# A two-block transformer kernel on one core: weights rounded in two halves of 1024 columns instead of one piece of 2048

## The reference, cut to what matters

```
def conv_ffn(h, w_up, conv_w, conv_b, w_down):
    u = h @ w_up
    ...
    return (jax.nn.silu(gate) * val) @ w_down

def swiglu(h, w13, w2):
    a, b = jnp.split(h @ w13, 2, axis=-1)
    return (jax.nn.silu(a) * b) @ w2
```

## Time and profile before

| | |
|---|---|
| median of 3 runs | 3355.73 us (3351.95 to 3360.63) |
| the profiled execution | 3357.11 us, of which its span (first to last instruction) is 3355.3 us |
| granted PE clock, mean | 0.995 of full |
| busy, share of the span | PE 98%, DVE 54%, ACT 37%, POOL 30% |
| weight loads | 298 of 1024 KB, median 4.8 us from issue to landing |

### The profile page before, as it was taken

How to read it: one execution, slowest core, us unless ns; L and a number is a source line. 1 busy time by engine, 2 the same in 40 slices (tenths; PEclk the granted TensorE clock), 3 DMA queues, 4 the chain that set the end, 5 groups by cost and what they waited for, 6 DMA issues and landing times.

```text
span 3355.3 us, 48284 instructions
## 1 busy us (share of the span) xinstructions
PE 3278.1 (98%) x17840; PEld 2804.2 (84%) x17840; DVE 1809.4 (54%) x2219; ACT 1247.2 (37%) x1627; POOL 1020.4 (30%) x505
## 2 busy tenths in 40 slices
PE   7989999999999999999999999999999999999999
PEld 6768888888888888998888877988888888998887
DVE  5467876553478766457645665664552255262222
ACT  4464333354444334443322445322242223442221
POOL 2112222221112222544434241343423332223332
PEclk9999999999999999999999999999999999999999
DMA  4202333321224333445544310454422243222222
GB/s 143 73 37 101 144 138 125 113 102 51 88 84 156 136 133 109 174 174 185 186 155 175 120 67 14 156 189 150 169 101 100 93 164 113 95 82 100 100 89 100
DMA packets 69901, 401.69 MB, mean 120 GB/s; under 512 B 7520, under 2 KB 10224, under 8 KB 31216
## 3 DMA queue, kind: packets, MB, share of 16 engines
q1 hardware_dynamic: 46400, 317.80, 26.2%
q10 hardware_dynamic: 23344, 81.73, 6.9%
HBM read 397.41 MB, written 2.10 MB: 119 GB/s over the span
## 4 chain that ended last, share of the span: by engine, by line
PE 90%; DVE 3%; ACT 3%; issue 2%; POOL 1%; DMA 1%; SPq 0%; DVEq 0%; ACTq 0%; POOLq 0%
PE banks L535 24%; PE banks L537 23%; PE banks L536 23%; PE banks L441 3%; PE banks L442 3%; PE banks L443 3%; PE banks L552 2%; PE banks L554 2%; PE banks L553 2%; ACT whi L970 1%; POOL wlo L2262 1%; PE banks L651 1%; DMA raw<-stream 1%; PE banks L886 1%; PE banks L873 1%
## 5 line engine op out<-in xcount | busy, mean ns | idle before, releaser
L2262 POOL TENSOR_TENSOR wlo<-raw,whi 128x512 fp32r<-128x512 f32 (+1 forms) x282 | 707.7, 2510 | 2025.7 <-ACT whi L970 2023.7
L535 PE MATMUL banks<-h_hi,whi 128*128 128x512 f32 (+1 forms) x2752 | 1040.2, 378 | 11.5 <-POOL wlo L2262 5.4
L536 PE MATMUL banks<-h_lo,whi 128*128 128x512 f32 (+1 forms) x2752 | 1034.2, 376 | 0.0
L537 PE MATMUL banks<-h_hi,wlo 128*128 128x512 f32 (+1 forms) x2752 | 1034.2, 376 | 0.0
L970 ACT ACTIVATE whi<-raw 128x2048 fp32r<-128x2048 f32 x281 | 536.9, 1911 | 527.8 <-PE banks L537 523.1
L1524 DVE TENSOR_TENSOR wlo<-raw,whi 128x1536 fp32r<-128x1536 f32 (+1 forms) x281 | 530.6, 1888 | 296.2 <-ACT whi L970 296.0
L535 PEld LDWEIGHTS banks<-h_hi,whi 128*128 128x128 f32 x2752 | 518.3, 188 | 112.2 <-issue 16.3
L536 PEld LDWEIGHTS banks<-h_lo,whi 128*128 128x128 f32 x2752 | 518.5, 188 | 94.3 <-issue 1.7
L537 PEld LDWEIGHTS banks<-h_hi,wlo 128*128 128x128 f32 x2752 | 518.5, 188 | 94.0
L535 PE MATMUL banks<-mid_hi,whi 128*128 128x512 f32 (+1 forms) x1136 | 424.6, 374 | 4.0 <-POOL wlo L2262 3.1
L536 PE MATMUL banks<-mid_lo,whi 128*128 128x512 f32 (+1 forms) x1136 | 424.0, 373 | 0.0
(11 more groups left out here) (287 smaller groups left out, 4029.6 us busy)
## 6 DMA issues: line engine op xcount, KB each, us to landing
raw<-stream SPq DMA_DIRECT2D x298, 1024.0 KB, 4.8
mraw<-mod_stream ACTq DMA_DIRECT2D x144, 512.0 KB, 3.4
x<-xT SPq DMA_DIRECT2D x8, 256.0 KB, 6.1
out<-x SPq DMA_DIRECT2D x8, 256.0 KB, 2.2
ka<-k_a ACTq DMA_DIRECT2D x1, 1600.0 KB, 8.6
ko<-k_odd ACTq DMA_DIRECT2D x1, 1152.0 KB, 5.3
crow<-c_rows ACTq DMA_DIRECT2D x1, 1024.0 KB, 7.1
cx<-ctxT SPq DMA_DIRECT2D x1, 1024.0 KB, 7.5
```

Source lines behind the costliest of these rows:

```text
L535: mm(o, hi, a_hi[:, kc, 0:T], start=(kc == 0), stop=False)
L536: mm(o, hi, a_lo[:, kc, 0:T], start=False, stop=False)
L537: last = mm(o, lo, a_hi[:, kc, 0:T], start=False, stop=(kc == K - 1))
L2262: G.tensor_tensor(wlo[:, slot, wd:], raw[:, slot, wd:], whi[:, slot, wd:].bitcast(F32), ALU.subtract)\
```

## The change

ACT rounds a slab in two instructions of 1024 columns each. The first raises a new semaphore `whi_half`, the second raises `whi_done`. POOL's part of `wlo` moves from the last columns to the first ones (0 to 511, in `ctx_ffn` 0 to 255) and waits for `whi_half` alone. DVE's part becomes two instructions: the rest of the first half (512 columns, in `ctx_ffn` 768) after `whi_half`, and the whole second half (1024 columns) after `whi_done`; `wlo_done` comes with the second. The same is done in `split_extra`. PE and SP wait for what they waited for before. The first two slabs of the program are rounded as before, only their columns are shared out anew. A DVE wait that was there twice goes.

```diff
+HW = SLAB // 2
...
-def dve_part(s):
+def pool_part(s):
     first, count = PLAN["ctx_ffn"]
-    return SLAB - (WPOOL // 2 if first <= s < first + count else WPOOL)
+    return WPOOL // 2 if first <= s < first + count else WPOOL
...
+        whi_half = sem("whi_half")
...
-                    A(whi[:, s % 2, :], raw[:, s % 2, :], ACT.Copy).then_inc(whi_done, 1)
+                    A(whi[:, s % 2, 0:HW], raw[:, s % 2, 0:HW], ACT.Copy).then_inc(whi_half, 1)
+                    A(whi[:, s % 2, HW:], raw[:, s % 2, HW:], ACT.Copy).then_inc(whi_done, 1)
...
                 if s + 2 < NSLAB:
+                    dve.wait_ge(whi_half, s + 1 + i2)
+                    dve.wait_ge(slab_done, s + 1 + i2)
+                    w = slice(pool_part(s), HW)
+                    V.tensor_tensor(wlo[:, s % 2, w], raw[:, s % 2, w], whi[:, s % 2, w].bitcast(F32), ALU.subtract)
                     dve.wait_ge(whi_done, s + 3 + i2)
-                    dve.wait_ge(slab_done, s + 1 + i2)
-                    w = slice(0, dve_part(s))
-                    V.tensor_tensor(wlo[:, s % 2, w], raw[:, s % 2, w], whi[:, s % 2, w].bitcast(F32),
+                    V.tensor_tensor(wlo[:, s % 2, HW:], raw[:, s % 2, HW:], whi[:, s % 2, HW:].bitcast(F32),
                                     ALU.subtract).then_inc(wlo_done, 1)
...
-            def split_w(slot, whi_at, done_at, wd=WD):
-                pool.wait_ge(whi_done, whi_at)
-                if done_at is not None:
-                    pool.wait_ge(slab_done, done_at)
-                G.tensor_tensor(wlo[:, slot, wd:], raw[:, slot, wd:], whi[:, slot, wd:].bitcast(F32), ALU.subtract)\
+            def split_w(slot, half_at, done_at, wd):
+                pool.wait_ge(whi_half, half_at)
+                pool.wait_ge(slab_done, done_at)
+                G.tensor_tensor(wlo[:, slot, 0:wd], raw[:, slot, 0:wd], whi[:, slot, 0:wd].bitcast(F32), ALU.subtract)\
                     .then_inc(wlo_pool_done, 1)
```

More of the change, by code:

```diff
@@ L988, in split_extra @@
                 act.wait_ge(raw_loaded[s % 2], 16 * (s // 2 + 1))
-                A(w_hi(s), raw[:, s % 2, :], ACT.Copy).then_inc(whi_done, 1)
+                A(w_hi(s)[:, 0:HW], raw[:, s % 2, 0:HW], ACT.Copy).then_inc(whi_half, 1)
+                A(w_hi(s)[:, HW:], raw[:, s % 2, HW:], ACT.Copy).then_inc(whi_done, 1)
             def load_ln_exp():
@@ L1533, in split_extra @@
             def split_extra(s):
+                dve.wait_ge(whi_half, s - 1)
+                V.tensor_tensor(w_lo(s)[:, WPOOL:HW], raw[:, s % 2, WPOOL:HW], w_hi(s)[:, WPOOL:HW].bitcast(F32),
+                                ALU.subtract)
                 dve.wait_ge(whi_done, s + 1)
-                V.tensor_tensor(w_lo(s)[:, 0:WD], raw[:, s % 2, 0:WD], w_hi(s)[:, 0:WD].bitcast(F32),
+                V.tensor_tensor(w_lo(s)[:, HW:], raw[:, s % 2, HW:], w_hi(s)[:, HW:].bitcast(F32),
                                 ALU.subtract).then_inc(wlo_done, 1)
@@ L1862, in _ @@
             dve.wait_ge(whi_done, 2)
-            V.tensor_tensor(wlo[:, 1, 0:WD], raw[:, 1, 0:WD], whi[:, 1, 0:WD].bitcast(F32), ALU.subtract)\
+            V.tensor_tensor(wlo[:, 1, WPOOL:], raw[:, 1, WPOOL:], whi[:, 1, WPOOL:].bitcast(F32), ALU.subtract)\
                 .then_inc(wlo_done, 1)
@@ L2249, in _ @@
             G = nc.gpsimd
-            WD = SLAB - WPOOL
             step = [0]
@@ L2320, in _ @@
                 .then_inc(wlo_pool_done, 1)
-            split_w(1, 2, None)
+            pool.wait_ge(whi_done, 2)
+            G.tensor_tensor(wlo[:, 1, 0:WPOOL], raw[:, 1, 0:WPOOL], whi[:, 1, 0:WPOOL].bitcast(F32), ALU.subtract)\
+                .then_inc(wlo_pool_done, 1)
             splits(slab_of("even_in"), 13)
```

14 lines of the change are left out of this document (6 added, 8 removed).

## The result

| | before | after |
|---|---|---|
| median | 3355.47 us (3351.95 to 3360.63, 4 runs) | 3333.9 us (3331.68 to 3336.98, 4 runs) |
| profiled execution | 3357.11 us | 3331.68 us |
| its span | 3355.3 us | 3329.9 us |
| granted PE clock, mean | 0.995 | 0.996 |

The ratio of the times is 0.9936, with a 95% interval of 0.9924 to 0.9949. The direction, the mechanism and most places were forecast; the size was not. The gain of 21.5 us is a third larger than the sum of 16.3 us, and 3333.9 lies 0.1 us under the low end of the range, 3334.0.

A forecast was written before the change was run, and what follows sets the result against it. PE, busy 3278.1 of 3355.3 us, was taken as the bound, so only its waits could be won. Terms summed to 16.3 us, giving 3340.8 from 3357.11; the forecast was 3340.5, range 3334 to 3350.

The forecast's parts named there:

- the down rounds of `ctx_ffn`: Rounds paced by a loop through three engines; each turn 0.5 us shorter, gaining 2.6 (first) and 3.2 (second and third).
- costs that did not come: Starts of attention stages, where PE waits with a rounding or split ahead: 0.1 to 0.3 us each, -0.8 in all.
- the up slabs: Up slabs of `ctx_ffn`: four PE waits, 3.0 us in all, nearly vanish as the chain shortens by 0.9; gain 2.9.
- the `halved` waits: Four PE waits of 0.8 us in `halved` stretches, 3.8 in all: gain 0.9 each, 3.6 us.
- The forecast chain of 3.7 in `ctx_ffn`: From ACT's start to the end of `wlo`: 3.7 us instead of 4.63; 0.9 us taken off each chain.
- 954 and 964: PE's wait of 2.2 us and the 4.1 us behind it, for `ss`: gain 1.5 us in all.
- the waits for `ss`: Four other PE waits for DVE's `ss`: POOL's blocking goes; gain 2.3 us, within bounds 0 and 3.6.
- The clock as a rival: Half-clock stretch near 963 and dip near 1523 go, winning 3 to 4 us more: 3337; chance 0.10.
- The rule on the lockout: Trainium skill: two-input DVE and POOL instructions exclude each other entirely; gain about 0.75 us a chain, time 3343.6.
- GpSimd comes last again: In the split chain, POOL gets the port only after DVE's second instruction; about 3348 us; chance 0.18.
- It gains nothing: PE's waits put down to POOL could be for something else landing at the same time: 3356 us; chance 0.05.
- VectorE's queue becomes the bound: Modulated conv layers: DVE's added waiting exceeds its 1.35 us idle a slab; 3361, up to 3370; chance 0.05.

The follow-up runs named there:

- e5: Kernel before, with ACT rounding in two halves but DVE (one instruction) and POOL (first columns) both waiting for the second: 3357.65 us, ratio 1.0010.
- e1: Kernel after, but DVE waits for the whole rounding and does its part in one instruction: 3331.55 us, ratio 0.9941.
- e4: Kernel after measured and profiled once more, without an edit: 3333.5 us, ratio 0.9942.
- e2: Kernel after, but DVE takes the whole first half and POOL the last columns, waiting for `whi_done`: 3340.23 us, ratio 0.9960.
- e3: Kernel after, but ACT rounds 512 then 1536 columns; POOL takes the first piece, DVE the second in one instruction: 3329.51 us, ratio 0.9933.
- e9: Kernel after with POOL's part cut from 512 columns to 64 (32 in `ctx_ffn`): 3330.61 us, ratio 0.9924.

## Why the prediction was right, and where it was not

**In sum.** Direction and mechanism were right, and three terms of the sum were mis-sized. Of the 9.1 us by which the steps exceed the sum (25.4 less 16.3) 3.1 are the clock's and 0.9 the first load's, which the medians don't show in full. The rest is in the down rounds of `ctx_ffn` (1.9), in two waits put at nothing (1.5) and in costs that did not come (1.2); what is left nearly cancels (0.4 and 0.4 too little for the up slabs and `ss`, 0.5 too much for the `halved` waits). These three make 4.6 of the 5.2 us by which the medians' gain of 21.5 exceeds 16.3.

**Right: what bounds the kernel, and the chain.** PE does not wait in the 512-token feed-forward layers, before or after the earlier trace rows; most of the 25.4 us lies at the places of rows 2 and at their like. The forecast chain of 3.7 in `ctx_ffn` is 3.72, that of 4.0 with 512 columns is 4.01 in `ffn00`; in the conv layers it is 4.52, and no wait shows it. The order of the turns (DVE, POOL, DVE) holds, and e5 and e1 show that POOL's turn inside the rounding brings the gain by itself. The waits before lines 535 and 441, forecast at 3 and 1.5 us, are 2.3 and 1.4.

**Right: four waits of `halved` stretches, 954 and 964, the waits for `ss`.** 3.6, 1.5 and 2.3 us were forecast, and the steps are 3.1, 1.6 and 2.7. The steps for `ss` also settle the choice within 0 and 3.6: near the upper bound, where it was taken, and that choice had little behind it.

**Failed step: the down rounds of `ctx_ffn`.** 2.6 and 3.2 were forecast, 3.4 and 4.2 came. The prediction made the loop 0.5 us shorter, to 6.2 a turn (one slab), and took it for the bound in every slab. In the timeline of the first round after (the rows of rows 6):

```profile
1439.10 0.87 DVE L1659 SCALAR_TENSOR_TENSOR cx<-banks,gates,cx 128x256 f32<-128x256 f32 x2
...
1444.69 1.05 ACT L972 ACTIVATE whi<-raw 128x1024 fp32r<-128x1024 f32 x1
...
1445.22 0.87 DVE L1659 SCALAR_TENSOR_TENSOR cx<-banks,gates,cx 128x256 f32<-128x256 f32 x2
1446.00 1.37 DVE L1526 TENSOR_TENSOR wlo<-raw,whi 128x768 fp32r<-128x768 f32 x1
1447.29 1.21 DVE L1528 TENSOR_TENSOR wlo<-raw,whi 128x1024 fp32r<-128x1024 f32 x1
1448.43 0.47 DVE L2082 SCALAR_TENSOR_TENSOR stg<-x,modA,rstd 128x256 f32<-128x256 f32 x1
...
1445.81 0.74 POOL L2266 TENSOR_TENSOR wlo<-raw,whi 128x256 fp32r<-128x256 f32 x1 [5.38 <-ACT whi L972]
```

The loop is as forecast. A turn takes 6.12 us (1445.22 less 1439.10) where 6.2 was said, POOL goes first, and from ACT's start `stg` ends at 4.21 where 4.3 was said and rows 6 have 4.82. What failed is that the loop's excess over PE's 5.76 (17.28 / 3) must reach PE. At 6.12 it is 0.36 us a slab, 1.1 in three, and yet PE does not wait in the first round at all. That two slabs are ready when the round begins, and this lead covers the excess, fits the numbers; no experiment tested it. The measured part is: 3.2 us went there (20.47 less 17.28), not 2.6. At 6.75, before, the excess was 1.0 a slab. In the later rounds, with their slabs of 36 matmuls, 2.3 us of idle time remain (25.85 less 23.58), of 4.4. Their step of 4.2 also holds some of the clock near 1523: +1.5 there, and 0.9 of it given back by 1529.

**Failed step: the costs.** 0.8 us were set down for places where PE waits for ACT or DVE with a rounding ahead. The steps there come to 0.4 the other way, and 0.7 with e4. In the first pair they are mostly the clock's: +1.6 between 205 and 215, mostly while before is at half the clock and after is not, and -1.4 and -0.8 up to 250, where after has two such stretches and before none. e5 shows what the division costs where a chain reaches PE: 0.1 a chain, 3.9 us over the whole program. In its profile the stages' starts cost no more than that (-0.1 up to 250). The forecast 0.9 of each chain already holds the division's price, and at the other places none can be seen. Why they gain a little isn't shown.

**Failed step: two waits not read.** The list of waits of before has a line that was passed over, since it names no `wlo`:

```profile
PE banks L535 <- issue: 1.4, 2, 0.7
```

The timeline of before around the first of the two, at 319.67, PE, then DVE and POOL:

```profile
319.67 0.47 PE L535 MATMUL banks<-h_hi,whi 128*128 128x512 f32 x1 [0.70 <-issue]
...
316.95 2.62 DVE L1524 TENSOR_TENSOR wlo<-raw,whi 128x1536 fp32r<-128x1536 f32 x1
...
316.66 1.30 POOL L2262 TENSOR_TENSOR wlo<-raw,whi 128x512 fp32r<-128x512 f32 x1 [31.05 <-ACT whi L970]
```

DVE's 1536 columns take 2.62 instead of 1.76 because POOL was first, they end at 319.57, and PE starts at 319.67: the wait is for DVE's `wlo`, whatever the view calls it. It is the first slab of a conv layer behind a stage, and 994.65 is its twin. After, at the same matmul:

```profile
315.19 1.31 POOL L2266 TENSOR_TENSOR wlo<-raw,whi 128x512 fp32r<-128x512 f32 x1 [32.00 <-ACT whi L972]
...
316.42 0.68 DVE L1526 TENSOR_TENSOR wlo<-raw,whi 128x512 fp32r<-128x512 f32 x1
...
317.02 1.22 DVE L1528 TENSOR_TENSOR wlo<-raw,whi 128x1024 fp32r<-128x1024 f32 x1
...
318.34 0.47 PE L537 MATMUL banks<-h_hi,whi 128*128 128x512 f32 x1
```

POOL is done (316.50) as DVE starts, both of DVE's pieces are free, and no idle time is shown before the matmul: it starts 0.19 us after its neighbour instead of 0.99. Worth 0.80 us at each of the two, and e2, which puts POOL behind again, loses 0.95 at each.

**The clock as a rival.** It was set at 3337 and 0.10, as a case of its own. The low stretch around 963 shrank (3.3 us at 0.50 in the windows above, from 6.80 in rows 7), the one near 1523 went, so in this pair of profiles the rival held in part, along with the forecast. But the same kernel in e4 shows both how much of that is chance (8.40 us at 0.59 around 960) and that the gain does not depend on it. A clock case that can come true together with the forecast should have widened the range downwards by its 3 to 4 us. That, and the three terms above, is why a range with its low end at 3334.0 was too high. That it was missed by only 0.1 us is no merit: 3334.0 was chosen for the clock case, and the time came there by other terms.

**The rule on the lockout.** The sum with a loser that begins in full only at the winner's end was 13.5 us, 3343.6. The rows decide for the prediction's own price: POOL's 256 columns end 0.59 behind DVE, and DVE's 1024 columns 1.09 behind POOL, where they have 1.21 alone (1447.29 above).

**The other rivals.** "GpSimd comes last again" did not occur; built as e2 it gave 3340.2, not 3348: its chain ends as early in the feed-forward layers, and it loses mainly DVE's following steps and the first slabs of conv layers. "It gains nothing" is refuted by the intervals. "VectorE's queue becomes the bound" is refuted by 320.00 of 320.00. Not named, but near: weights that are loaded earlier, since `wlo` ends earlier. ACT's waits for loads were 4.7 us in all, and after, 518.1 of the 521.6 us of idle time before its first pieces are ended by PE, so little can come from there.

**Small slips.** DVE's own end in `ctx_ffn` was 4.05 us after ACT's start (1371.11 less 1367.06), not 3.95. DVE's two pieces cost 0.15 more than one (0.96 and 1.21 against 2.02), not 0.1. And of the 6.12 busy us at half the clock 2.7 went, not 3, at 0.21 against 0.12 us a matmul. None of them moves the sum.

**What stays open.** The attention stages add up to little, with steps of both signs whose causes were not taken apart. The 5.4 us by which e1 makes up its loss in `ctx_ffn` are of that kind. Whether e3 or e9 is faster than after needs more runs than were made.
